# Selector products from the first microsecond, and decay rates spread from four bands, at the start of a hybrid Hyena / attention / MoE kernel

## The reference, cut to what matters

```python
def _adaln(cond, w, b):
    mod = jax.nn.silu(cond) @ w + b
...
    h = jnp.sin(f_freq * (feat @ f_w1 + f_b1))
    h = jnp.sin(f_freq * (h @ f_w2 + f_b2))
    h = (h @ f_w3).astype(jnp.float32) * jnp.exp(-t * jnp.abs(decay).astype(jnp.float32))
```

## Time and profile before

| | us |
|---|---|
| median of 3 runs | 1037.05 (1036.37 to 1038.48) |
| the profiled execution's own time | 1036.07 |
| its span | 1034.3 |
| busy in the span: TensorE, DVE, POOL, ACT | 985.1, 713.4, 196.0, 189.3 |
| start of in_0 on TensorE | 39.03 |

### The profile page before, as it was taken

How to read it: one execution, slowest core, us unless ns; L and a number is a source line. 1 busy time by engine, 2 the same in 40 slices (tenths; PEclk the granted TensorE clock), 3 DMA queues, 4 the chain that set the end, 5 groups by cost and what they waited for, 6 DMA issues and landing times.

```text
span 1034.3 us, 28524 instructions
## 1 busy us (share of the span) xinstructions
PE 985.1 (95%) x11472; PEld 589.8 (57%) x11472; DVE 713.4 (69%) x1905; ACT 189.3 (18%) x443; POOL 196.0 (19%) x304
## 2 busy tenths in 40 slices
PE   7999999999999999999999999989999999999893
PEld 2555555565665666666655555565566665666451
DVE  6548883965765767777678996375566776777567
ACT  4342223112310000000150012463231000000003
POOL 0500000530131222222101000154012222222121
PEclk9999999999999999999999999999999999999897
DMA  9954565960889999799996478843088799999991
GB/s 363 423 210 163 213 238 221 387 212 28 334 343 423 425 421 414 309 424 421 421 423 243 174 324 325 303 117 91 1 317 329 314 420 425 416 408 420 423 383 61
DMA packets 36799, 318.29 MB, mean 308 GB/s; under 512 B 8402, under 2 KB 12690, under 8 KB 18803
## 3 DMA queue, kind: packets, MB, share of 16 engines
q1 hardware_dynamic: 26820, 298.87, 71.4%
q0 software_dynamic: 5776, 17.30, 4.8%
q10 hardware_dynamic: 4128, 1.05, 0.5%
HBM read 311.44 MB, written 5.77 MB: 307 GB/s over the span
## 4 chain that ended last, share of the span: by engine, by line
PE 84%; DVE 7%; DMA 5%; issue 2%; POOL 1%; ACT 1%; SPq 0%; DVEq 0%; ACTq 0%; POOLq 0%
PE bank L840 81%; DMA ring<-in_k_down 4%; POOL P L808 1%; PE bank L1362 1%; DMA group_row<-token_rows,rows_now 1%; DVE P L2263 1%; PE bank L892 1%; DVE st L2200 0%; PE bank L1060 0%; DVE x L2314 0%; PE bank L904 0%; PE bank L876 0%; DVE sc L2010 0%; DVE x L2315 0%; PE bank L884 0%
## 5 line engine op out<-in xcount | busy, mean ns | idle before, releaser
L840 PE MATMUL bank<-ring,xgT 128*32 128x256 f32 x4224 | 243.9, 381 | 7.1 <-issue 6.4
L840 PE MATMUL bank<-hT,ring 128*128 128x384 f32 x640 | 207.2, 486 | 0.0
L840 PEld LDWEIGHTS bank<-ring,xgT 128*32 128x32 f32 x4224 | 147.6, 110 | 94.7 <-issue 20.8
L840 PEld LDWEIGHTS bank<-hT,ring 128*128 128x128 f32 x640 | 121.4, 190 | 85.6 <-issue 1.8
L1765 DVE CUSTOM_DVE_ANT_0 ring<-ring,ring 128x1024 f32<-128x1024 f32 x112 | 137.1, 1224 | 3.4
L840 PE MATMUL bank<-ring,heT 128*32 128x256 f32 x2112 | 131.0, 386 | 5.9 <-DMA ring<-in_k_down 5.4
L2150 DVE TENSOR_TENSOR he<-sa,bank 128x64 f32<-128x64 f32 x132 | 26.6, 202 | 126.9 <-ACT sa L1599 126.9
L1599 ACT ACTIVATE sa<-bank 128x128 f32<-128x128 f32 x66 | 18.3, 278 | 421.9 <-PE bank L840 421.9
L840 PEld LDWEIGHTS bank<-ring,heT 128*32 128x32 f32 x2112 | 62.7, 110 | 56.0 <-DVE heT L2152 13.5
L840 PE MATMUL bank<-yt,ohT 32*128 32x256 bf16 x2448 | 80.5, 269 | 0.5 <-DVE yt L2184 0.3
L774 POOL DMA_INDIRECT group_row<-token_rows,rows_now x68 | 74.0, 1089 | 17.4 <-issue 17.1
(11 more groups left out here) (302 smaller groups left out, 1212.4 us busy)
## 6 DMA issues: line engine op xcount, KB each, us to landing
ring<-in_k_up SPq DMA_DIRECT2D x64, 2048.0 KB, 17.5
ring<-in_k_down SPq DMA_DIRECT2D x32, 2048.0 KB, 18.1
ring<-in_k_ada SPq DMA_DIRECT2D x14, 2048.0 KB, 17.1
ring<-in_k_seg SPq DMA_DIRECT2D x10, 2048.0 KB, 13.4
ring<-in_k_qkv SPq DMA_DIRECT2D x6, 2048.0 KB, 16.3
ring<-in_k_in SPq DMA_DIRECT2D x5, 2048.0 KB, 8.2
ring<-in_k_out SPq DMA_DIRECT2D x4, 2048.0 KB
bm<-in_na_bias SPq DMA_DIRECT2D x16, 256.0 KB, 3.2
```

The costliest lines, as they stand in the source:

```text
L840: return nc.tensor.matmul(out, lhsT, rhs, start=first, stop=last)
```

## The change

The single row of `ones` becomes `sel[128, 128]`, zero but for the rows 0, 32, 64 and 96, which are ones. POOL writes it in its first five instructions. The rates are loaded as four rows of 512 into the partitions 0, 32, 64 and 96 of `rates`, which DVE has set to zero; SP waits for that. Each spread is a product of 32 rows of `sel` and of `rates`, so that the four lie in four different row bands of the array. DVE takes the absolute value over all 128 partitions of 512. All four spreads come right behind mlp0. ACT copies them out behind the first sine; the four copies of DVE are gone. TensorE gets products of `sel` with itself, whose results nobody reads: five before everything, ten behind the spreads, eight behind mlp1. The load of `skip`, which lies over `sel` and `rates`, waits for cond0 instead of the last spread.

```diff
-        ones = at("ones", [1, 128], RS + 12288)
+        sel = at("sel", [128, 128], RS + 12288)
+        rates = at("rates", [128, 512], RS + 12288 + 512)
...
+            sp.wait_ge(rates_zero, 1)
+            sp.dma_start(rates[0:128:32, :], bass.AP(A["hy_decay"].tensor, A["hy_decay"].offset, [[512, 4], [1, 512]])).then_inc(dabs_in, 16)
...
-                    sp.wait_ge(group_ready, G_AT["decay3"] + 1)
+                    sp.wait_ge(group_ready, G_AT["cond0"] + 1)
...
+            nc.gpsimd.memset(sel[:], 0.0).then_inc(ones_ready, 1)
+            pool.wait_ge(ones_ready, 1)
+            for c in range(4):
+                nc.gpsimd.memset(sel[32 * c:32 * c + 1, :], 1.0).then_inc(ones_ready, 1)
...
+            def selectors_turned(n):
+
+                for _ in range(n):
+                    mm(ps[7][:, 0:128], sel[:], sel[:])
+
+            pe.wait_ge(ones_ready, 5)
+            selectors_turned(5)
             pe.wait_ge(mlp_in, 16)
             mm(bank(G_AT["mlp0"])[0:FH, 0:TOK], fw1, feat).then_inc(group_ready, 1)
             pe.wait_ge(row_ready, 1)
-            pe.wait_ge(ones_ready, 1)
...
-                mm(bank(G_AT[f"decay{c}"])[:, :], ones[:], dabs[0:1, 512 * c:512 * c + 512]).then_inc(group_ready, 1)
+                q = slice(32 * c, 32 * c + 32)
+                mm(bank(G_AT[f"decay{c}"])[:, :], sel[q, :], rates[q, :]).then_inc(group_ready, 1)
...
-            spread_decay(0)
-            spread_decay(1)
+            for c in range(4):
+                spread_decay(c)
+            selectors_turned(10)
             pe.wait_ge(mh_ready, 1)
             mm(bank(G_AT["mlp1"])[:, 0:TOK], fw2, mh1[:]).then_inc(group_ready, 1)
-            spread_decay(2)
-            spread_decay(3)
+            selectors_turned(8)
...
+            for c in range(4):
+                g = G_AT[f"decay{c}"]
+                wait_group(act, g)
+                nc.scalar.activation(dabs[:, 512 * c:512 * c + 512], ps[bank_of(g)][:, :], ACT.Copy).then_inc(evacuated[g % 8], 1)
...
+            v.memset(rates[:], 0.0).then_inc(rates_zero, 1)
...
-            row = dabs[0:1, :]
-            v.scalar_tensor_tensor(out=row, in0=row, scalar=-1.0, in1=row, op0=ALU.mult, op1=ALU.max).then_inc(row_ready, 1)
+            v.scalar_tensor_tensor(out=rates[:], in0=rates[:], scalar=-1.0, in1=rates[:], op0=ALU.mult, op1=ALU.max).then_inc(row_ready, 1)
...
-                for c in (2 * n, 2 * n + 1):
-                    g = G_AT[f"decay{c}"]
-                    wait_group(dve, g)
-                    v.tensor_copy(dabs[:, 512 * c:512 * c + 512], ps[bank_of(g)][:, :]).then_inc(evacuated[g % 8], 1)
```

More of the change, by code:

```diff
@@ L90 @@
 _at = 0
-for _name, _n in [("mlp0", 1), ("decay0", 1), ("decay1", 1), ("mlp1", 1), ("decay2", 1), ("decay3", 1),
+for _name, _n in [("mlp0", 1), *[(f"decay{c}", 1) for c in range(4)], ("mlp1", 1),
                   ("cond0", 1), ("filt0", 4), ("cond0_sum", 1), ("cond1", 1), ("filt1", 4), ("cond1_sum", 1),
@@ L407, in build @@
         ones_ready, in0_half, row_ready = sem("ones_ready"), sem("in0_half"), sem("row_ready")
+        rates_zero = sem("rates_zero")
         rows_landed = sem("rows_landed")
@@ L635, in _ @@
             sp.dma_start(mlp[:], A["k_mlp"]).then_inc(mlp_in, 16)
-            sp.dma_start(dabs[0:1, :], bass.AP(A["hy_decay"].tensor, A["hy_decay"].offset, [[0, 1], [1, 2 * D]])).then_inc(dabs_in, 16)
+            sp.wait_ge(rates_zero, 1)
+            sp.dma_start(rates[0:128:32, :], bass.AP(A["hy_decay"].tensor, A["hy_decay"].offset, [[512, 4], [1, 512]])).then_inc(dabs_in, 16)
             for d in range(2):
@@ L1727, in link @@
                 dve.wait_ge(dve_step, steps[0])
+            v.memset(rates[:], 0.0).then_inc(rates_zero, 1)
             v.memset(scond[:], 0.0).then_inc(scond_zero, 1)
             v.memset(credit[:, 7:8], LN_EPS).then_inc(eps_ready, 1)
-            v.memset(ones[:], 1.0).then_inc(ones_ready, 1)
             dve.wait_ge(first_in, 16)
```

## The result

| | before | changed | ratio, 95% interval |
|---|---|---|---|
| median of 20 runs each, us | 1036.17 (1032.73 to 1038.48) | 1039.97 (1034.74 to 1043.26) | 1.0034 [1.0023, 1.0046] |

The changed kernel is slower by 0.34%, some 3.5 us. The forecast was 1036.4 us with no change that can be told as the likeliest case, in a range up to 1038.2; it stood on a median of 1037.05 for the kernel before, so its range ended 1.2 us above that kernel, and the miss doesn't come from the base. The single runs of the changed kernel reach from 1034.7 to 1043.3 us, so one execution says little about the median: the profiled one took 1035.71 us (span 1033.9), at the lower end.

What follows compares the result with a forecast made beforehand. TensorE's chain was taken as the bound, its input projection's start shifting everything behind. A gain of 2.3 us at the first conditioning sum less 1.7 for a clock fall made -0.6 us: 1036.4 us, range 1033.7 to 1038.2.

Steps and rivals of the forecast that it cites:

- Five products ahead of mlp0: TensorE's start: the products end at 3.6 to 4.6 us against mlp0's table at 4.16; taken as no delay.
- The absolute value: DVE, before the first argument: 0.75 us replaces 2.28, so the first sine ends 0.6 us earlier.
- The spreads: TensorE behind mlp0: four side by side take 1.9 us, from 5.6 to 7.5.
- Ten products ahead of mlp1: TensorE behind the spreads: clock rises there, products end at 11.0 us, mlp1 0.5 later but quicker, second sine 0.2 earlier.
- The decay path: ACT behind the second sine: table load at 16.2 us instead of 17.11, decays end at 19.5, `arow` at 20.0.
- The gain at the sum: First conditioning sum on TensorE: starts at 20.0 us instead of 22.27, a gain of 2.3 us.
- The load of cond0: Queue of loads: estimated to land at 13.5 us, hiding the eight products but for 0.4 us.
- What is late next: TensorE's gap from 18.1 to 21.0 us: clock falls to half, cond1 and the taps behind lose 1.7 us.
- rival 1: Clock rises early and doesn't fall in the gap: gain of 2.3 us kept, 1034.7 us; chance 0.37.
- The step that failed: Start of the input projection on TensorE, 39.20 us before: whatever shifts it was taken to shift everything behind it.
- a wait for a load: Behind the input projection's start: losing the 2 to 3 us gained there again would show the prediction wrong.
- The products' worth: Selector products on TensorE: raise the clock early, mlp1 0.95 us instead of 1.64, cond0 1.9 instead of 3.64.

Runs made afterwards that it cites:

- e7: Changed kernel without its 23 selector products, with 12 tiny products ahead of mlp0 (48 instructions): 1035.61 us, ratio 1.0005.
- e2: Changed kernel without any of its 23 selector products: 1034.64 us, ratio 0.9997 against the kernel before.
- e11: Changed kernel without its 23 selector products, with four repetitions of a DVE step of the second argument: 1037.32 us, ratio 1.0012.
- e5: Changed kernel without its selector products, with 23 tiny products ahead of mlp0 in their place (92 instructions): 1038.02 us, ratio 1.0031.
- e9: Kernel before, with 23 tiny products ahead of cond0 (92 instructions): 1041.59 us, ratio 1.0054.
- e8: Changed kernel without selector products, with 36 tiny products, 12 ahead of mlp0 and 24 ahead of cond0 (144 instructions): 1034.01 us, ratio 0.9994.
- e12: Kernel before, with 36 tiny products ahead of cond0 (144 instructions): 1038.38 us, ratio 1.0029.
- e6: Changed kernel with 41 tiny products added behind the first filter taps (256 added instructions in all): 1036.63 us, ratio 1.0018.

## Why the prediction was wrong

The steps in its own order.

*Five products ahead of mlp0*: 0 to 0.4 us late, taken as 0. It was 0.27 (4.43 against 4.16). Within the bounds.

*The absolute value*: 0.69 us for 0.75. The first argument started at 6.10 for 5.72, chiefly since mlp0 started 0.27 us later than before.

*The spreads*: taken as 1.9 us from 5.6. They are 2.0, from 5.90 to 7.92. The estimate by the Trainium skill's page TensorE: Matmul & The Clock Gate, Part 3, had been 2.4; against the 7.5 us one after another this is 3.7 times, so the trace doesn't agree with the page's 3.07.

*Ten products ahead of mlp1*: taken to end at 11.0; they ended at 11.47, at the late end of what was said. mlp1 took 0.91 us (0.95). The decay path followed, as late as mlp1: table load 16.64 (16.2), `arow` 19.84 with the sum at 20.56 (20.0). The gain at the sum is 1.7 us for 2.3; most of the 0.6 between them is mlp1's 0.47. (The load of cond0, estimated to land at 13.5, landed at 12.4 in e7 and at 14.6 in e2, where TensorE waited for it.)

*What is late next*: the fall of the clock in the gap, 1.7 us. It didn't come in either profile of the changed kernel, both with 1.90 us of idle time and 1.02 us of narrow products in a row. The windows of the changed kernel behind the gap (start and end, length, busy time with counts by engine, granted clock, DMA share, GB/s):

```profile
20.50:23.90 3.40, 3.34 (x26) 1.69 (x28) 3.04 (x8) 3.40 (x3) 1.87 (x2) 1.00 1.02 439
```

The mechanism exists, though. The kernel without products and with a delay (e11) has the same gap of 1.90 us, at 19.65, with another 1.22 of idle time ahead of its taps, and there the windows give:

```profile
21.00:22.50 1.50, 0.95 (x8) 0.97 (x8) 1.33 (x4) 1.50 (x2) 0.00 (x0) 1.00 1.08 459
...
24.00:25.50 1.50, 1.50 (x10) 0.15 (x2) 1.27 (x3) 1.28 (x2) 1.01 (x2) 0.50 1.02 437
```

```profile
25.35 2.63 PE L848 MATMUL bank<-fw,mh 64*128 64x512 f32 x8
```

The clock fell to its lower level in the stretch behind the gap; cond1 took 2.92 us instead of 1.92 and the taps 2.63 instead of 1.99, 1.6 us in all, close to the forecast's 1.7. e5 fell behind 0.99 us of waiting. So the price was right, and whether it is paid was not to be told from the length of the gap: one gap of 1.90 us was followed by a fall and two weren't. As a term of the changed kernel it should have been 0. That is rival 1, given 0.37; by itself it would have made the kernel 1.6 us faster.

*The step that failed* stands in the first part: "Whatever shifts the start of that projection shifts everything behind it." The shift of 1.64 us reached 294 us whole and was 0.38 us at the last expert product of the profiled execution; over many executions the changed kernel ends 3.5 us later than the one before. The sum had no term for what 92 more instructions do to the code behind them. The prediction named a loss further on only as "a wait for a load"; what its runs show are stops of TensorE without a load, and beside them up to 1.6 us of waiting for gathered rows at the second expert group (e9; 0.5 us in the changed kernel). The error had been open to reading: the chain of the kernel before has its stops of 1.09 and 1.12 us under "issue" in the same stretch, and nothing else in the trace accounts for them.

*The products' worth.* The forecast gave them the quick mlp1 and the quick cond0. Both came, and e2 shows that neither counts at in_0.

**What is shown and what is argued.** Shown: the products alone make the loss (e2 against the changed kernel); it comes back without their work (e5, in part by a fall of the clock, and in the kernel before e9); it doesn't grow with the amount that is added (e8 below e5, clear of both intervals; e12 below e9, with intervals that overlap; e6 ends no later than the changed kernel); it isn't a floor that absorbs gains (e9); and the stops stand at fixed counts of TensorE's instructions, so that added ones move them to other products and 256 bring them back (the table of places). Argued, from the times in the DMA records and from the distance of some 122 records: that a stop is a wait for a block of program text. Open: why some fetches stop TensorE and others don't, and why the same place stops for 0.15 us in one execution and for 0.98 in another; how much of the 5.2 us behind in_0 the stops make up, for the profiles with 92 instructions have 1.1 to 3.4 us in layer 0's experts; and the 1.7 us that the kernel without products loses behind in_0, which may be the changed counts on DVE and ACT or no more than the uncertainty. No version beat the kernel before by more than can be told: the best, e8, is at 0.9994 [0.9979, 1.0009].

## What to carry to other kernels

Instructions that do nothing but keep an engine busy are not free where they hide: they lengthen the program, and in a later stretch of many short products stops of 1 us appear or vanish with their number. Before pricing an edit by its own place, look in the chain for "issue" pieces of about 1 us, count the matmul records ahead of them, and look for the instruction queue's packets near them; where there are some, an early gain of 1 or 2 us is below what the edit's instruction count can take away or give. Test such an edit with the same count of instructions and no work in them, and judge by the median of many runs: one profile of this kernel was 4 us off its median. Follow a lead through the whole trace, too: read at one product alone it was nought, at another 2.5 us.

## What I had not expected of the hardware

- TensorE stops for 0.1 to 1.8 us amid products with nothing to wait for, 3 to 9 times in the 240 us of layer 0's experts, and 2.8 to 8.0 us in sum over fourteen profiles. One of 1.6 to 1.8 us, right ahead of the first expert product, is in all of them.
- The others stand at fixed counts of instructions: behind 1575 to 1588, 1697 to 1704, 1819 to 1830 and 1946 to 1948 matmul records with 0 to 256 instructions added ahead. A stop with 0.43 us of idle time printed (at 500.36) cost 1.1 us.
- The number of added instructions changed the time by more than their work: 92 of them 5.6 us and 144 of them 3.0 us, in the same place of the same kernel.
- Nearly the same gap may or may not bring the clock down: 1.90 us idle and 1.02 us of narrow products were followed by 1.00 in the changed kernel and by 0.50 in e11, 0.99 and 1.02 us by 0.50 in e5, and 1.30 and 1.07 us in the earlier trace rows by 0.50.
- Tiny products in the place of a gap didn't keep the clock up: behind 41 of them in 2.76 us (e6) it was at 0.50 from 22.2 to 28.9 us.
- Four products of 32 rows and 512 columns in four bands took 2.0 us together, where one of one row takes 1.9 (two in 3.77).
- Executions of one program spread by 8.5 us, 0.8% (the changed kernel's 20 runs).
